# Half products that accumulate in PSUM, weights requested between two spills, copies between token parts: an input projection on one core

## The chip, the cores and the metric

The kernel runs on one core of one Trainium2 chip. The metric is the device time of one execution in microseconds. The program of a core runs on several engines side by side: TensorE (PE, matmuls, with PEld for its weight loads), VectorE (DVE), ScalarE (ACT), GpSimd (POOL), and SyncE (SP), which here only requests DMA transfers. They wait for one another through semaphores.

## What is computed

One inference step of a decoder trunk of two layers, for 1040 prompt rows (16 meta tokens and 1024) and 8 samples of 4 rows, 1072 tokens in all. The layer's input projection is the part that matters here:

```python
hn = _rmsnorm(x, pre_g)
proj = jnp.einsum('bld,de->ble', hn, w_in)      # D_MODEL = 1024 -> EVEN_IN or ODD_IN features
# even layer (A): q, k, v, og, ig, fg, z, xr, gr = split(proj)
#   mLSTM heads on q, k, v, gated by sigmoid(og) and silu(z); RG-LRU on xr, gr
# odd layer (C):  q, k, v, r, alow = split(proj)
#   gated linear attention on q, k, v, gated by silu(r)
mix = ...                                       # the recurrences
y = x + _rmsnorm(jnp.einsum('ble,ed->bld', mix, w_out), post_g)
```

## The kernel before

Each layer has a projection stage and a mixing stage. Every fp32 matrix product is made of three passes over a high and a low part of each operand: high with high, high with low, low with high. The low part is made on DVE by subtracting the high part, which ACT makes by a copy with rounding; this is called a split.

The first tiles of a projection (gates, LRU inputs, q, k) are computed directly (`Projection`, line 471): the features of a tile are 128, the contraction goes over 8 blocks of 128, and the tokens are cut in three. The remaining 32 tiles of 128 features, in each layer, are computed in 16 pairs by `HalfProducts`. A pair is an upper and a lower tile of features. The contraction is cut in two halves, the tokens are cut in two halves, and so a pair is a 2 x 2 block product, which is made from seven half products instead of eight. They are numbered 1 to 7. Products 1 and 2 need the upper weights, products 5, 6 and 3 need the sums of weights, products 7 and 4 need the lower weights and a sum. Each needs a token part: parts 1, 2 and 4 are sums made ahead, part 3 is made last and is stored over a part of the normed tokens (`t3_sum`, `t3_his`, `t3_lows`). One half product is 24 matmuls of 268 columns on line 624: 2 column halves, 4 blocks, 3 passes.

PE takes the products of a pair in the order that `order` gives, and puts them in turn in four places of PSUM of two banks each (`out`). It waits before a product until the one that lay in its place four products ago has been read (`wait_read`). ACT copies product 1 from PSUM (line 650; in pair 0 products 5, 4 and 1), and DVE adds all others (line 657) into the stage tiles `upper` and `lower`. The upper tile is finished by the add of product 3 (or 2), the lower one by that of product 4 (or 7).

For each pair the weights are loaded from HBM (`load`, line 542, two transfers of 512 KB, one for each of the two raw buffers `pa_w_raw` or `pc_w_raw`). `sum_weights` makes three sums on DVE (lines 552 to 557), `split_upper_hi` (ACT, line 565), `split_upper_lo` (DVE, line 569), `split_sums_hi` (ACT, line 575), `split_sums_lo` (DVE, line 579), `split_lower_hi` (ACT, line 587) and `split_lower_lo` (DVE, line 591) split them. A raw buffer may be loaded again when its split and the sums are done.

A finished tile is gated or scaled in place or with a helper tile and then spilled to HBM by two transfers (lines 989 and 990, 2511 and 2512). In layer A the pairs are 4 of kind k (scaled on ACT, line 1131), 4 of og (sigmoid on ACT), 4 of z (sigmoid on ACT, line 1136, then multiplied on DVE, line 1254) and 4 of v (plain). In layer C the first 8 pairs are gated (sigmoid on ACT, line 2601, multiplied on DVE, line 2696), and the last 8 are plain. A stage tile is written again only when its spill has landed.

The order of the work on each engine is written out by hand: `copies` and `finish` for ACT, `sums_of` for DVE, `products` for PE, and the loop over pairs on SP, where the weights of pair p + 1 are requested at the top of pair p, ahead of both of its spills. Ahead of the first of them, in layer A, SP requests three small transfers (lines 1008 to 1010).

Of the kernel before, what the change touches and what calls it, by code (L numbers as in the profile page):

```python
# [35 lines left out]
H = 4  # L36
# [455 lines left out]
class HalfProducts:  # L492
# [100 lines left out]
    def order(self, p):  # L593

        return "1265374" if p else "5412637"
# [114 lines left out]
    def t3_his(self, act):  # L710
        for k in range(KH):
            act.wait_ge(self.t_sum, 3 * KH + k + 1)
            act.activation(self.S.XT_hi[:, k, HC:T], self.temps[2 * (k % 2)], ACT.Copy).then_inc(self.t_hi_ready, 1)
# [11 lines left out]
    def copies(self, act, p, upper, lower):  # L725

        if p == 0:
            act.wait_ge(self.spilled[1], 32 * self.before)
            self.copy(act, p, 5, lower[1])
            self.copy(act, p, 4, lower[0])  # L730
        act.wait_ge(self.spilled[0], 32 * (self.before + p))
        self.copy(act, p, 1, upper[0])

    def sums_of(self, dve, p, upper, lower, more, between):

        def into(x, y, after):

            dve.wait_ge(self.added, after)
            dve.tensor_tensor(x, x, y, ALU.add).then_inc(self.added, 1)
        if p:  # L740
            self.split_lower_lo(dve, p)
            dve.wait_ge(self.copied, 3 + p)
            dve.wait_ge(self.spilled[1], 32 * (self.before + p))
            self.add(dve, p, 6, lower[0], upper[0], 0)
            self.add(dve, p, 2, upper[0], upper[0], 1)
            if more:
                self.split_upper_lo(dve, p + 1)
            self.add(dve, p, 5, lower[1], lower[0], 1)
# [2803 lines left out]
```

## Time and profile before

| | us |
|---|---|
| median of 3 runs | 2098.87 (2097.29 to 2101.58) |
| the profiled execution, its own time | 2098.2 |
| its span, first to last instruction | 2096.4 |
| PE busy with matmuls | 2027.8 (97%) |
| DVE busy | 1239.6 (59%) |
| ACT busy | 798.4 (38%) |
| mean granted clock of TensorE | 0.984 of full |

The profile is of one execution. Its times are counted from the span's start. A row of the timeline gives start, duration, engine, line, operation, output and inputs, and in brackets how long the engine stood idle before it and who ended that. Matmuls overlap in PE, so their durations (0.29 us) are longer than the distance of their starts.

### The profile page before, as it was taken

To read this page: it belongs to the slowest core of one execution; us is meant where nothing else is said; L and a number is where in the kernel's file an instruction comes from. 1 tells how busy PE (TensorE), PEld (TensorE's weight loads), DVE (VectorE), ACT (ScalarE), POOL (GpSimd) and SP (SyncE) were. 2 spreads that over 40 slices of the span, in tenths; PEclk is the share of its full clock that TensorE was granted. 3 is DMA by queue.
4 is the path that set the end of the run, shared out by engine and by line. 5 is a ranking of instruction groups with operands and counts; after the bars stand their busy time and mean duration, and the time that the engine had idled before them with its cause. 6 is when DMAs were issued, how large, how long until landed. Compare 5 with 4: busy or idle time off the path is not lost. (4 is left out here: it accounts for less than half of the span.)

```text
span 2096.4 us, 33284 instructions
## 1 busy us (share of the span) xinstructions
PE 2027.8 (97%) x12862; PEld 1803.7 (86%) x12862; DVE 1239.6 (59%) x2206; ACT 798.4 (38%) x1501; POOL 320.3 (15%) x442
## 2 busy tenths in 40 slices
PE   7999999999999799999979999999999799999998
PEld 7999999999999677787659999999999677777774
DVE  5466676645564666666646557676655465455544
ACT  5555543323231544444345344332212343333323
POOL 0000000000000532242210000000000452323222
PEclk9999999999999999999979999999999899999999
DMA  3121232443333754555332332444433544545442
GB/s 141 56 63 51 65 103 76 149 155 93 114 102 102 244 175 161 173 166 190 102 133 76 98 88 84 139 137 134 117 95 112 181 173 165 183 164 182 161 155 73
DMA packets 211496, 268.92 MB, mean 128 GB/s; under 512 B 49396, under 2 KB 157172, under 8 KB 209304
## 3 DMA queue, kind: packets, MB, share of 16 engines
q1 hardware_dynamic: 211352, 266.95, 39.9%
q8 instruction: 97, 1.59, 0.3%
q14 instruction: 47, 0.39, 0.1%
HBM read 172.72 MB, written 94.18 MB: 127 GB/s over the span
## 5 line engine op out<-in xcount | busy, mean ns | idle before, releaser
L657 DVE TENSOR_TENSOR pa_stage<-pa_ps,pa_stage 128x536 f32<-128x536 f32 x110 | 77.0, 712 | 119.3 <-PE pa_ps L624 111.0
L657 DVE TENSOR_TENSOR pc_stage<-pc_ps,pc_stage 128x536 f32<-128x536 f32 x110 | 77.0, 712 | 100.4 <-PE pc_ps L624 79.3
L471 PE MATMUL pa_ps<-a_XT_hi,pa_w_hi 128*128 128x358 f32 x576 | 133.2, 340 | 0.3 <-PEq L204 0.3
L471 PE MATMUL pa_ps<-a_XT_hi,pa_w_lo 128*128 128x358 f32 x576 | 125.9, 327 | 0.0
L471 PE MATMUL pa_ps<-a_XT_lo,pa_w_hi 128*128 128x358 f32 x576 | 125.8, 326 | 0.0
L624 PE MATMUL pc_ps<-c_XT_hi,pc_w_hi 128*128 128x268 f32 x384 | 110.2, 287 | 0.0
L624 PE MATMUL pa_ps<-a_XT_hi,pa_w_lo 128*128 128x268 f32 x384 | 110.1, 287 | 0.0
L624 PE MATMUL pc_ps<-c_XT_hi,pc_w_lo 128*128 128x268 f32 x384 | 110.1, 287 | 0.0
L624 PE MATMUL pc_ps<-c_XT_lo,pc_w_hi 128*128 128x268 f32 x384 | 110.1, 287 | 0.0
L624 PE MATMUL pa_ps<-a_XT_lo,pa_w_hi 128*128 128x268 f32 x384 | 110.0, 286 | 0.0
L624 PE MATMUL pa_ps<-a_XT_hi,pa_w_hi 128*128 128x268 f32 x384 | 109.8, 286 | 0.0
L1553 PE MATMUL mc_ps<-mc_wout_hi,mc_mix_hi 128*128 128x512 f32 x256 | 105.9, 414 | 4.0 <-POOL mc_mix_lo L3301 4.0
L471 PEld LDWEIGHTS pa_ps<-a_XT_hi,pa_w_hi 128*128 128x128 f32 x576 | 100.2, 189 | 5.9 <-issue 0.6
L1553 PE MATMUL ma_ps<-ma_wout_hi,ma_mix_hi 128*128 128x512 f32 x256 | 104.9, 410 | 0.0
L1553 PE MATMUL mc_ps<-mc_wout_hi,mc_mix_lo 128*128 128x512 f32 x256 | 101.4, 396 | 0.0
L1553 PE MATMUL mc_ps<-mc_wout_lo,mc_mix_hi 128*128 128x512 f32 x256 | 101.0, 394 | 0.0
L1553 PE MATMUL ma_ps<-ma_wout_hi,ma_mix_lo 128*128 128x512 f32 x256 | 100.5, 393 | 0.0
L1553 PE MATMUL ma_ps<-ma_wout_lo,ma_mix_hi 128*128 128x512 f32 x256 | 100.2, 391 | 0.0
L471 PEld LDWEIGHTS pa_ps<-a_XT_hi,pa_w_lo 128*128 128x128 f32 x576 | 99.6, 189 | 0.0
L471 PEld LDWEIGHTS pa_ps<-a_XT_lo,pa_w_hi 128*128 128x128 f32 x576 | 99.4, 189 | 0.0
L3294 POOL TENSOR_TENSOR mc_state<-mc_state,gf 128x512 f32<-128x512 f32 x72 | 74.8, 1060 | 86.8 <-DVE mc_state L3211 86.8
L3211 DVE TENSOR_TENSOR mc_state<-mc_ps,mc_state 128x512 f32<-128x512 f32 x64 | 41.2, 686 | 76.8 <-PE mc_ps L2981 76.1
(581 smaller groups left out, 6000.8 us busy)
## 6 DMA issues: line engine op xcount, KB each, us to landing
pa_w_raw<-in_w_a SPq DMA_DIRECT2D x57, 512.0 KB, 4.6
pc_w_raw<-in_w_c SPq DMA_DIRECT2D x49, 512.0 KB, 4.5
scr_c<-pc_stage SPq DMA_DIRECT2D x48, 512.0 KB, 3.2
scr_a<-pa_stage SPq DMA_DIRECT2D x40, 512.0 KB, 3.2
mc_sample_state<-in_s SPq DMA_DIRECT2D x32, 512.0 KB, 4.6
out_s_s<-mc_sample_state SPq DMA_DIRECT2D x32, 512.0 KB, 2.8
ma_sample_state<-in_c SPq DMA_DIRECT2D x32, 257.0 KB, 4.1
out_c_s<-ma_sample_state SPq DMA_DIRECT2D x32, 257.0 KB, 2.6
```

The costliest lines, as they stand in the source:

```text
L471: ins = pe.matmul(self.ps[:, 3 * s + t, 0:TC], w[:, k, :], x[:, k, t * TC:(t + 1) * TC], start=(k == 0 and j == 0), stop=(k == KT - 1 and ...
L624: ins = pe.matmul(bank[:, half, :], a[:, k, :], b[:, k, cols], start=(k == 0 and j == 0), stop=(k == KH - 1 and j == 2))
L657: dve.tensor_tensor(dst, self.out(p, product), x, ALU.add).then_inc(self.added, 1)
L1553: ins = pe.matmul(ps[:, 6 + half, :], m[:, at, :], w, start=first and j == 0, stop=last and j == 2)
L3211: ins = dve.tensor_tensor(cst[:, n % H, d, :], ps[:, 4 + d, :], cst[:, n % H, d, :], ALU.add)
L3294: ins = pool.tensor_tensor(cst[:, h, d, :], cst[:, h, d, :], factor, ALU.mult)
```

## The change

The half products no longer have four places in turn. In a pair, products 1, 6, 7 and 4 accumulate on top of one another in one place, and products 5 and 3 in another; product 2 has the place that the next pair's product 1 will have. A product that opens a place starts with `start=True`, the others add to what lies there. The order of the products becomes 1 2 6 5 7 3 4, and 5 1 2 6 3 7 4 in pair 0. ACT now copies products 1, 6, 5 and 4, each time the sum so far, and DVE adds products 2, 7 and 3. So a product that adds to a place waits until the sum so far has been read there: 6 for the copy of 1, 7 for the copy of 6, 3 for the copy of 5, 4 for the add of 7.

On ACT a pair is now: the split of its own lower weights, the last step of the pair before, copy 1, the split of the next pair's upper weights, copies 6 and 5, the split of the next sums, the last step of the upper tile, copy 4. In pair 0 it is copy 5, a high part of token part 3, copy 1, another, then the same; two of the four high parts stay ahead of the pairs. On DVE it is the low part of the sums and of the lower weights, the last step of the pair before, add 2, the weight sums of the next pair, add 7, the low part of the next upper weights, add 3 (in pair 0 add 7 comes last).

SP requests the weights of pair 1 where it did before, and those of pair p + 2 between the upper and the lower spill of pair p.

```diff
@@ -592,7 +592,7 @@
 
     def order(self, p):
 
-        return "1265374" if p else "5412637"
+        return "1265734" if p else "5126374"
 
     def at(self, p, product):
 
@@ -600,20 +600,20 @@
 
     def out(self, p, product):
 
-        s = (self.at(p, product) + 1) % 4
+        s = {1: p % 2, 6: p % 2, 7: p % 2, 4: p % 2, 2: 1 - p % 2, 5: 2, 3: 2}[product]
         return self.G.ps[:, 2 * s:2 * s + 2, 0:HC // 2]
 
-    def wait_read(self, eng, p, product):
-
-        copied = {1: 3 + p} if p else {5: 1, 4: 2, 1: 3}
-        added = {6: 1, 2: 2, 5: 3, 3: 4, 7: 6, 4: 7} if p else {6: 1, 2: 4, 3: 5, 7: 7}
-        if product in copied:
-            eng.wait_ge(self.copied, copied[product])
-        else:
-            eng.wait_ge(self.added, 7 * p + added[product])
+    def wait_copied(self, eng, p, what):
+
+        eng.wait_ge(self.copied, 4 * p + ("1654" if p else "5164").index(str(what)) + 1)
+
+    def wait_added(self, eng, p, product):
+
+        eng.wait_ge(self.added, 3 * p + ("273" if p else "237").index(str(product)) + 1)
 
     def product(self, pe, p, product):
 
+        opens = product in (1, 2, 5)
         w, t = {1: ("A11", "B11"), 2: ("A12", "B21"), 3: (2, "B22"), 4: ("A22", 4), 5: (0, 1), 6: (1, 2), 7: ("S3", 3)}[product]
         bank = self.out(p, product)
         passes = [(self.weights(w, lo_w), self.tokens(t, lo_t)) for lo_w, lo_t in ((0, 0), (0, 1), (1, 0))]
@@ -621,17 +621,33 @@
             cols = slice(half * HC // 2, (half + 1) * HC // 2)
             for k in range(KH):
                 for j, (a, b) in enumerate(passes):
-                    ins = pe.matmul(bank[:, half, :], a[:, k, :], b[:, k, cols], start=(k == 0 and j == 0),
-                                    stop=(k == KH - 1 and j == 2))
+                    ins = pe.matmul(bank[:, half, :], a[:, k, :], b[:, k, cols], start=(opens and k == 0 and j == 0),
+                                    stop=(k == KH - 1 and j == 2), skip_group_check=True)
         ins.then_inc(self.done, 1)
 
-    def products(self, pe, p):
+    def products(self, pe, p, hook=None):
         for i, name in enumerate(self.order(p)):
-            q = 7 * p + i
-            if q == 2:
-                pe.wait_ge(self.G.psum_free[0], (self.first + 1) // 2)
-            if q >= 4:
-                self.wait_read(pe, (q - 4) // 7, int(self.order((q - 4) // 7)[(q - 4) % 7]))
+            if i == 4 and hook:
+                hook()
+            if name == "1":
+                if p:
+                    self.wait_added(pe, p - 1, 2)
+                else:
+                    pe.wait_ge(self.G.psum_free[0], (self.first + 1) // 2)
+            elif name == "2":
+                if p:
+                    self.wait_copied(pe, p - 1, 4)
+            elif name == "6":
+                self.wait_copied(pe, p, 1)
+            elif name == "5":
+                if p:
+                    self.wait_added(pe, p - 1, 3)
+            elif name == "7":
+                self.wait_copied(pe, p, 6)
+            elif name == "3":
+                self.wait_copied(pe, p, 5)
+            else:
+                self.wait_added(pe, p, 7)
             if name in "12":
                 pe.wait_ge(self.upper_ready, p + 1)
             elif name in "563":
@@ -644,17 +660,28 @@
                     pe.wait_ge(self.t_ready, 1)
             self.product(pe, p, int(name))
 
-    def copy(self, act, p, product, dst):
-
+    def copy(self, act, p, product, tiles):
+
+        upper, lower = tiles
+        dst, s = {1: (upper[0], 0), 6: (upper[1], 0), 5: (lower[1], 1), 4: (lower[0], 1)}[product]
+        act.wait_ge(self.spilled[s], 32 * (self.before + p))
         act.wait_ge(self.done, self.at(p, product))
         act.activation(dst, self.out(p, product), ACT.Copy).then_inc(self.copied, 1)
 
-    def add(self, dve, p, product, dst, x, after):
-
+    def add(self, dve, p, product, tiles):
+
+        upper, lower = tiles
+        dst, copied = {2: (upper[0], 1), 7: (lower[1], 5), 3: (upper[1], 6)}[product]
+        self.wait_copied(dve, p, copied)
         dve.wait_ge(self.done, self.at(p, product))
-        if after:
-            dve.wait_ge(self.added, 7 * p + after)
-        dve.tensor_tensor(dst, self.out(p, product), x, ALU.add).then_inc(self.added, 1)
+        dve.tensor_tensor(dst, self.out(p, product), dst, ALU.add).then_inc(self.added, 1)
+
+    def wait_tile(self, eng, p, m):
+
+        self.wait_added(eng, p, (3, 7)[m])
+        self.wait_copied(eng, p, (6, 4)[m])
+        if m == 0:
+            self.wait_added(eng, p, 2)
 
     def t_sums(self, dve, i):
 
@@ -722,55 +748,51 @@
         dve.wait_ge(self.t3_used, KH)
         dve.sem_inc(self.t_ready, 1)
 
-    def copies(self, act, p, upper, lower):
-
...
+    def act_pair(self, act, p, tiles, more, finish, after_first=lambda: None, late=lambda: None):
+
         if p:
+            self.split_lower_hi(act, p)
+            finish(p - 1, 1)
+            self.copy(act, p, 1, tiles)
+            after_first()
+        else:
+            self.copy(act, p, 5, tiles)
+            self.t3_his(act, 2)
+            self.copy(act, p, 1, tiles)
+            self.t3_his(act, 3)
+        if more:
+            self.split_upper_hi(act, p + 1)
+        self.copy(act, p, 6, tiles)
+        if p:
+            self.copy(act, p, 5, tiles)
+        late()
+        if more:
+            self.split_sums_hi(act, p + 1)
+        finish(p, 0)
+        self.copy(act, p, 4, tiles)
+        if not more:
+            finish(p, 1)
+
+    def dve_pair(self, dve, p, tiles, more, finish, middle=lambda: None):
+
+        if p:
+            self.split_sums_lo(dve, p)
             self.split_lower_lo(dve, p)
-            dve.wait_ge(self.copied, 3 + p)
-            dve.wait_ge(self.spilled[1], 32 * (self.before + p))
...
+            finish(p - 1, 1)
+        self.add(dve, p, 2, tiles)
+        middle()
+        if more:
+            self.sum_weights(dve, p + 1)
+        if p:
+            self.add(dve, p, 7, tiles)
+        if more:
             self.split_upper_lo(dve, p + 1)
-            self.add(dve, p, 3, upper[1], lower[1], 3)
-            self.sum_weights(dve, p + 1)
...
+        self.add(dve, p, 3, tiles)
+        if not p:
+            self.add(dve, p, 7, tiles)
+        finish(p, 0)
+        if not more:
+            finish(p, 1)
 
 
 A_KINDS = ("k", "og", "z", "v")
@@ -1009,11 +1031,10 @@
                 sp.dma_start(row_d, S.rrow).then_inc(finished, 16)
                 sp.dma_start(gain_d.rearrange("o (k p) -> p (o k)", p=P), S.vecs[:, V_PRE_C:V_PRE_C + KT],
                              allow_slow_non_contiguous=True).then_inc(finished, 16)
+                for s in range(2):
+                    HP.load(sp, 1, s)
                 for p in range(NPAIR):
                     kind, h = kind_of(p)
-                    if p + 1 < NPAIR:
-                        for s in range(2):
-                            HP.load(sp, p + 1, s)
                     if 1 <= p <= w_out.tiles // 2:
                         sp.wait_ge(rows_turned, 1)
                         sp.wait_ge(HP.t_ready, 1)
@@ -1024,8 +1045,12 @@
                             sp.wait_ge(spilled[s], A_SPILLED[0])
                         load_first_head(sp)
                     for m in range(2):
+                        if m and p + 2 < NPAIR:
+                            for s in range(2):
+                                HP.load(sp, p + 2, s)
                         if kind == "v":
-                            spill(HP.added, HP.ready(p)[m], m, h, A_SLOT[kind] + m)
+                            HP.wait_tile(sp, p, m)
+                            spill(HP.done, 7 * p + 6 + m, m, h, A_SLOT[kind] + m)
                         else:
                             spill(final[m], p + 1, m, h, A_SLOT[kind] + m)
                 sp.wait_ge(lru_spilled, 16 * 2 * 8)
@@ -1118,7 +1143,8 @@
                         gate_rows_act_out(act)
                     if k == 6:
                         HP.split_sums_hi(act, 0)
-                HP.t3_his(act)
+                HP.t3_his(act, 0)
+                HP.t3_his(act, 1)
                 act.preload_act_table_set('sigmoid_and_others')
 
                 def finish(p, m):
@@ -1126,7 +1152,7 @@
                     kind, h = kind_of(p)
                     if kind == "v":
                         return
-                    act.wait_ge(HP.added, HP.ready(p)[m])
+                    HP.wait_tile(act, p, m)
                     if kind == "k":
                         act.activation(flat[m][:, 0:T], flat[m][:, 0:T], ACT.Copy, scale=0.0625).then_inc(final[m], 1)
                     elif kind == "og":
@@ -1136,16 +1162,9 @@
                         act.activation(z_sig, flat[m][:, 0:T], ACT.Sigmoid).then_inc(sigmoid_ready, 1)
                 for p in range(NPAIR):
                     more = p + 1 < NPAIR
-                    if p == 3 * H:
+                    if p == 3 * H + 1:
                         act.preload_act_table_set('natural_log_exp_and_others')
-                    HP.copies(act, p, upper, lower)
-                    if more:
-                        HP.split_upper_hi(act, p + 1)
-                        HP.split_sums_hi(act, p + 1)
-                    finish(p, 0)
-                    if more:
-                        HP.split_lower_hi(act, p + 1)
-                    finish(p, 1)
+                    HP.act_pair(act, p, (upper, lower), more, finish)
 
             @block.vector
             def _(dve):
...
@@ -2530,11 +2548,13 @@
                 for i in range(8):
                     pair(i)
                 spill(qk_ready, 16, 0, 3, 3)
+                def next_weights(p):
+                    if p + 2 < NPAIR:
+                        for s in range(2):
+                            HP.load(sp, p + 2, s)
+                next_weights(-1)
                 for p in range(NPAIR):
                     gated, h, d = head_of(p)
-                    if p + 1 < NPAIR:
-                        for s in range(2):
-                            HP.load(sp, p + 1, s)
                     if 1 <= p <= w_out.tiles // 2:
                         sp.wait_ge(HP.t_ready, 1)
                         w_out.load(sp, p - 1)
@@ -2545,10 +2565,14 @@
                         load_first_head(sp)
                     if gated:
                         spill(u_ready, p + 1, 0, h, 8 + d)
+                        next_weights(p)
                         spill(l_ready, p + 1, 1, h, 9 + d)
                     else:
-                        spill(HP.added, HP.ready(p)[0], 0, h, 4 + d)
-                        spill(HP.added, HP.ready(p)[1], 1, h, 5 + d)
+                        for m in range(2):
+                            HP.wait_tile(sp, p, m)
+                            spill(HP.done, 7 * p + 6 + m, m, h, 4 + d + m)
+                            if m == 0:
+                                next_weights(p)
 
             @block.scalar
             def _(act):
...
```

## Rows read from the trace of the kernel before

**Rows 1.** The page, part 1: busy us, share of the span, count.

```profile
PE 2027.8 (97%) x12862; PEld 1803.7 (86%) x12862; DVE 1239.6 (59%) x2206; ACT 798.4 (38%) x1501; POOL 320.3 (15%) x442
```

**Rows 2.** Windows of both layers' half products, line 624 alone.

```profile
core 0: us, PE busy (x) PEld busy (x), PEclk, DMA share, GB/s
354.00:687.40 333.40, 333.33 (x2687) 333.14 (x2688) 1.00 0.38 116
1304.60:1637.80 333.20, 332.92 (x2688) 332.74 (x2688) 1.00 0.39 119
```

**Rows 3.** Windows of two pairs of layer A; after PEld come DVE, ACT, POOL.

```profile
541.70:562.60 20.90, 20.90 (x171) 20.90 (x170) 14.10 (x17) 6.36 (x7) 0.00 (x0) 1.00 0.35 103
...
666.70:687.40 20.70, 20.70 (x169) 20.70 (x168) 6.78 (x9) 1.68 (x2) 0.00 (x0) 1.00 0.19 54
```

**Rows 4.** Timeline of PE in layer C's pair 0.

```profile
1316.92 0.39 PE L624 MATMUL pc_ps<-pc_t_hi,pc_w_sums_hi 128*128 128x268 f32 x1 [0.24 <-ACT pc_stage L650]
```

**Rows 5.** Timeline of PE, first matmul of the half products in A and C.

```profile
353.99 0.29 PE L624 MATMUL pa_ps<-pa_t_hi,pa_w_sums_hi 128*128 128x268 f32 x1
...
1304.63 0.29 PE L624 MATMUL pc_ps<-pc_t_hi,pc_w_sums_hi 128*128 128x268 f32 x1
```

**Rows 6.** Timeline of ACT in layer A's pair 0: the next pair's upper split.

```profile
372.07 1.06 ACT L565 ACTIVATE pa_w_hi<-pa_w_raw 128x1024 fp32r<-128x1024 f32 x1 [5.51 <-DMA pa_w_raw<-in_w_a]
```

**Rows 7.** Timeline of SP ahead of layer A's pair 1.

```profile
358.78 0.39 SPq L1010 DMA_DIRECT2D scr_g<-vecs  x1
```

**Rows 8.** The tile view of pa_w_raw, window 359 to 365: requests and landings.

```profile
L542 SPq DMA_DIRECT2D pa_w_raw<-in_w_a x2: 363/440/517, 359.3 to 359.9; - x2
...
DMA to landing us min/median/max: 12.8/13.1/13.5
```

**Rows 9.** Timeline of DVE in pair 0 of A (three) and C (one).

```profile
355.34 1.22 DVE L569 TENSOR_TENSOR pa_w_lo<-pa_w_raw,pa_w_hi 128x1024 fp32r<-128x1024 f32 x1 [3.65 <-ACT pa_w_hi L565]
...
374.93 0.68 DVE L552 TENSOR_TENSOR pa_w_sums<-pa_w_raw 128x512 f32<-128x512 f32 x1
...
377.46 1.33 DVE L657 TENSOR_TENSOR pa_stage<-pa_ps,pa_stage 128x536 f32<-128x536 f32 x2
...
1307.25 1.22 DVE L569 TENSOR_TENSOR pc_w_lo<-pc_w_raw,pc_w_hi 128x1024 fp32r<-128x1024 f32 x1
```

**Rows 10.** Timeline of ACT at the end of one pair of layer A.

```profile
414.30 1.49 ACT L575 ACTIVATE pa_w_sums_hi<-pa_w_sums 128x1536 fp32r<-128x1536 f32 x1 [7.93 <-DVE pa_w_sums L557]
415.69 1.08 ACT L1131 ACTIVATE pa_stage<-pa_stage 128x1072 f32<-128x1072 f32 x1
417.04 1.06 ACT L587 ACTIVATE pa_w_hi<-pa_w_raw 128x1024 fp32r<-128x1024 f32 x1 [0.26 <-PE pa_ps L624]
```

**Rows 11.** Timeline of DVE and SP in layer C: a gate, its spill, the spill's landing.

```profile
1353.14 1.33 DVE L2696 SCALAR_TENSOR_TENSOR pc_stage<-pc_stage,vecs,first_head_c 128x1072 f32<-128x1072 f32 x1 [1.17 <-ACT first_head_c L2601]
...
1358.06 1.53 DVE L657 TENSOR_TENSOR pc_stage<-pc_ps,pc_stage 128x536 f32<-128x536 f32 x2 [2.21 <-DMA scr_c<-pc_stage]
...
1354.50 0.37 SPq L2511 DMA_DIRECT2D scr_c<-pc_stage  x1
```

**Rows 12.** Timeline of SP and ACT in layer A: the slowest upper spill.

```profile
585.47 0.38 SPq L989 DMA_DIRECT2D scr_a<-pa_stage  x1
...
590.61 0.62 ACT L650 ACTIVATE pa_stage<-pa_ps 128x536 f32<-128x536 f32 x1 [3.09 <-DMA scr_a<-pa_stage]
```

**Rows 13.** PE's timeline after a long gap, and windows with the granted clock.

```profile
1663.62 0.80 PE L1553 MATMUL mc_ps<-mc_wout_hi,mc_mix_hi 128*128 128x512 f32 x1 [4.03 <-POOL mc_mix_lo L3301]
...
1665.50:1668.90 3.40, 3.40 (x9) 2.31 (x7) 0.00 (x0) 0.00 (x0) 3.40 (x6) 0.50 0.00 0
1669.00:1672.40 3.40, 3.40 (x21) 2.49 (x21) 1.67 (x3) 0.26 (x1) 2.86 (x6) 1.00 0.00 0
...
1316.00:1320.00 4.00, 3.76 (x31) 3.54 (x30) 0.00 (x0) 2.82 (x5) 0.00 (x0) 1.00 0.00 0
```

**Rows 14.** The page, part 6: requests, count, KB each, median us to landing.

```profile
pa_w_raw<-in_w_a SPq DMA_DIRECT2D x57, 512.0 KB, 4.6
```

More of the change, by code:

```diff
@@ L708, in t3_sum, with t3_his @@
         dve.tensor_tensor(x, x, y, ALU.add).then_inc(self.t_sum, 1)
[L710 to L713, printed above, removed]
+    def t3_his(self, act, k):
+        act.wait_ge(self.t_sum, 3 * KH + k + 1)
+        act.activation(self.S.XT_hi[:, k, HC:T], self.temps[2 * (k % 2)], ACT.Copy).then_inc(self.t_hi_ready, 1)
     def t3_lows(self, dve):
@@ L723, in t3_lows @@
         dve.sem_inc(self.t_ready, 1)
-    def copies(self, act, p, upper, lower):
[L727 to L739, printed above, removed]
-        if p:
-            self.split_lower_lo(dve, p)
-            dve.wait_ge(self.copied, 3 + p)
-            dve.wait_ge(self.spilled[1], 32 * (self.before + p))
-            self.add(dve, p, 6, lower[0], upper[0], 0)
-            self.add(dve, p, 2, upper[0], upper[0], 1)
-            if more:
-                self.split_upper_lo(dve, p + 1)
-            self.add(dve, p, 5, lower[1], lower[0], 1)
-            self.add(dve, p, 3, upper[1], lower[1], 3)
-            if more:
-                self.sum_weights(dve, p + 1)
-            self.add(dve, p, 7, lower[1], lower[1], 4)
-            self.add(dve, p, 7, lower[0], lower[0], 3)
-        else:
-            dve.wait_ge(self.copied, 3)
-            self.add(dve, p, 6, upper[1], upper[0], 0)
-            into(lower[1], upper[1], 1)
-            into(lower[0], upper[1], 1)
-            self.add(dve, p, 2, upper[0], upper[0], 1)
-            self.split_upper_lo(dve, p + 1)
-            self.add(dve, p, 3, upper[1], lower[1], 3)
-            self.sum_weights(dve, p + 1)
-            self.add(dve, p, 7, lower[1], lower[1], 5)
-            self.add(dve, p, 7, lower[0], lower[0], 3)
-        if more:
-            self.split_sums_lo(dve, p + 1)
-        between()
-        if p:
-            self.add(dve, p, 4, lower[0], lower[0], 6)
@@ L771, in ready @@
-    def ready(self, p):
-        return 7 * p + 4 if p else 5, 7 * p + 7
+    def act_pair(self, act, p, tiles, more, finish, after_first=lambda: None, late=lambda: None):
+        if p:
+            self.split_lower_hi(act, p)
[19 more added lines that the diff above has]
+            finish(p, 1)
@@ L1258, in _ @@
                 for p in range(NPAIR):
-                    if p and kind_of(p - 1)[0] == "z":
-                        z_gate(p - 1, 1)
-                    HP.sums_of(dve, p, upper, lower, p + 1 < NPAIR,
-                               (lambda: z_gate(p, 0)) if kind_of(p)[0] == "z" else (lambda: None))
+                    HP.dve_pair(dve, p, (upper, lower), p + 1 < NPAIR, z_gate)
             @block.gpsimd
@@ L2594, in _, with sigmoid @@
                 HP.split_upper_hi(act, 0)
[L2595 removed]
+                HP.t3_his(act, 0)
+                HP.t3_his(act, 1)
                 act.preload_act_table_set('sigmoid_and_others')
[L2598 to L2601 removed]
+                def sigmoid(p, m):
+                    if head_of(p)[0]:
+                        HP.wait_tile(act, p, m)
+                        act.wait_ge(sig_read, 2 * p + m)
+                        act.activation(sig, flat[m][:, 0:T], ACT.Sigmoid).then_inc(sig_ready, 1)
                 for p in range(NPAIR):
                     gated, h, d = head_of(p)
[L2604 removed]
+                    if p == 9:
                         act.preload_act_table_set('natural_log_exp_and_others')
[L2606 to L2616 removed]
+                    HP.act_pair(act, p, (upper, lower), p + 1 < NPAIR, sigmoid)
             @block.vector
@@ L2689, in _, with gate @@
                 HP.t3_lows(dve)
-                def gate(p, m, x):
+                def gate(p, m):
                     gated, h, d = head_of(p)
+                    if not gated:
+                        return
+                    x = flat[m]
                     dve.wait_ge(sig_ready, 2 * p + m + 1)
@@ L2701, in _ @@
                 for p in range(NPAIR):
-                    if p and head_of(p - 1)[0]:
-                        gate(p - 1, 1, flat[1])
-                    HP.sums_of(dve, p, upper, lower, p + 1 < NPAIR, (lambda: gate(p, 0, flat[0])) if head_of(p)[0] else (lambda: None))
+                    HP.dve_pair(dve, p, (upper, lower), p + 1 < NPAIR, gate)
             @block.tensor
```

21 lines of the change are left out of this document (2 added, 19 removed).

## The prediction

> **What bounds the kernel now.** I read the page's busy line first: the TensorE (PE) has work for 97% of the span [rows 1]. The reader is to see that a change can gain only where PE stands still, and can lose wherever it makes PE stand still. Then I cut out the two stretches that the change touches, the half products of both layers (line 624), with the windows view: 333.40 us and 333.20 us with 333.33 and 332.92 us of matmul in them [rows 2]. So at most 0.07 + 0.28 = 0.35 us of idle can be removed there. In layer C's pair 0 PE's timeline names one wait, 0.24 us, for an ACT copy [rows 4]. A third look is at single pairs: VectorE (DVE) is busy 14.10 of 20.90 us in one and 6.78 of 20.70 us in another, and PE starts its matmuls at the same pace in both (171 in 20.90 us, 169 in 20.70 us) [rows 3]. Taking adds off DVE gives PE nothing. Hence the working is about one question: which waits does the new order put in front of PE?
>
> One unit is needed throughout: 333.4 us / 2688 matmuls = 0.124 us, so a product (24 matmuls) takes 2.98 us and a pair (7 products) 20.83 us.
>
> **Removed work.** A pair loses four DVE adds and gets three ScalarE (ACT) copies more. An add takes 0.72 us, of two in a row the second starts about 0.62 us after the first (line 657, 1.33 us for two) [rows 9]; a copy takes 0.62 us [rows 12]. Both lie under 20.83 us of matmul, with DVE and ACT idle for a third of it or more [rows 3]: worth nothing. If the cover were gone, three copies would cost 1.9 us a pair.
>
> **Pair 0 of layer A, product 7.** PE starts at 353.99 [rows 5]; the new order is 5 1 2 6 3 7 4, so product 7 is due at 353.99 + 5 x 2.98 = 368.87. It now accumulates where product 6 lies, so it waits for ACT's copy of 6. In ACT's queue that copy stands behind the split of the next pair's upper weights (line 565), and ACT's rows stand in the order of its program. In the trace that split starts at 372.07, after 5.51 us of waiting for the weights' transfer [rows 6]. The transfer isn't moved: it is requested at 359.3 and 359.9, behind the small transfers that end with the one of line 1010 [rows 7], and lands 12.8 and 13.5 us later [rows 8], so at 372.1 and 373.4. Before, nothing that PE needed soon stood behind it. Now: split 372.07 to 373.13, its successor starting about 0.1 us before its end as in [rows 10] (414.30 + 1.49 against 415.69), copy 373.03 to 373.65, PE about 0.05 us later, at 373.7. Stall: 373.7 - 368.87 = 4.8 us.
>
> **The same pair, product 4.** It accumulates where product 7 has just been written, so it waits for DVE's add of 7, the last product before it. That add has 2.98 us of cover in later pairs, where product 3 stands between, and none in pair 0. Product 7 ends at 373.7 + 2.98 = 376.7. DVE has to do the next pair's weight sums first, which need both transfers: from 373.4, 2.53 us as in the trace (374.93 to 377.46), then the upper weights' low part (about 1.15 us), add 3 (0.62 us until the next starts), add 7 (0.72 us) [rows 9]: 373.4 + 2.53 + 1.15 + 0.62 + 0.72 = 378.4. PE goes on at 378.5 instead of 376.7: 1.8 us more. Together 4.8 + 1.8 = 6.6 us.
>
> **Pair 0 of layer C.** Here the weights are requested without small transfers ahead, and nothing waits for them. Product 1 moves from third place to second and needs the upper weights' low part, which DVE starts at 1307.25 and ends 1.22 us later [rows 9]: 1308.5 against 1304.63 + 2.98 = 1307.6 [rows 5]; 0.9 us. Layer A has the same step, but there the part is ready at 355.34 + 1.22 = 356.56 [rows 9], before product 1 is due at 356.97. Product 4 again waits for add 7, with nothing in between: an engine hears of PE's end 0.26 us after it [rows 10], the add takes 0.72 us, the way back some 0.05 us: 1.0 us. Sum for C: 1.9 us.
>
> **The clock.** An idle PE of 4.8 us has no like in these stages, but has one later: PE waits 4.03 us and goes on at 1663.62, and in 1665.50 to 1668.90 the granted clock is 0.50 (1.2 of 2.4 GHz); at 1669.00 it is 1.00 again [rows 13]. The short gap in layer C (0.24 us idle [rows 4]) left 1.00 around it [rows 13]. So I take half clock for the same 1669.0 - 1663.6 = 5.4 us after product 7 starts: 21.8 of its 24 matmuls at twice 0.124 us, 2.2 at 0.124, end 379.4 instead of 376.7. The add of 7 is free by then, and product 4 starts at 379.4 + 0.26 + 0.72 + 0.05 = 380.4, 1.9 us later than without. Bounds: 0 (clock kept) and 1.9 us; I take 1.9, since the gap of 4.03 us is the nearest row. The gaps of 0.9 and 1.0 us in C I put at no loss of clock, by the row around C's gap.
>
> **Every later pair.** With start T, product 6 is third, due at T + 5.95, and waits for the copy of product 1, which waits until the pair before has spilled its upper tile. In the gated pairs (8 in C, 4 of z in A) that chain starts at product 3's end, now the sixth, at T - 2.98: +0.26 to ACT, the sums' split (1.39 us until the next start), sigmoid 1.08 [rows 10], the gate on DVE 1.33, then the spill's request (1354.50 for a gate that began at 1353.14, so 1.36) [rows 11]. Request: T - 2.98 + 0.26 + 1.39 + 1.08 + 1.36 = T + 1.1. From the request to the wait's end it is 3.56 us where two weight transfers follow at once, as they will now [rows 11]: T + 4.7, copy 0.62, T + 5.35. Cover left: 0.6 us, so no stall. One landing in the trace took 5.14 us (585.47 to 590.61) [rows 12]; such a one would cost 5.14 - 3.56 - 0.6 = 1.0 us. I put this at 0, with 12 x 0.4 = 5 us as its upper bound for transfers that slow each other by 1 us.
>
> The request of weights between the two spills stands on the sync queue (SP) ahead of the lower spill. It waits for the lower weights' split, which DVE ends at about T + 4.1 (after the gate's end at T + 1.1, the low part of the sums, an estimated 1.8 us from 1.22 us for two thirds of the elements, then 1.22 us [rows 9]); the lower tile's gate follows and ends at T + 5.4, so nothing is held there. An ungated tile is held some 3 us, but its buffer is needed only by the copy of product 5 at T + 11.9 + 0.26, and the spill lands by T + 9. The weights land about T + 9, and their sums (2.53 us) end before DVE's add of 7 is due at T + 15.1. Nothing queued there is late.
>
> **The stages' ends.** The last step is a copy of 0.62 us in place of an add of 0.72 us: -0.1 us at each, left out.
>
> **Sum.** 6.6 + 1.9 (A) + 1.9 (C) - 0.35 (idle of before removed) = 10.05 us. The profiled execution took 2098.2 us (span 2096.4 and 1.8 around it), 0.67 us under the median of the runs shown and inside their spread. 2098.2 + 10.05 = 2108.
>
> **Rivals.**
>
> *The weights come in time (no change).* If both landed before 368.87 - 0.67 - 0.96 = 367.2 (the copy with its way to PE, and the split), product 7 would start on time. Left are add 7 in both layers (1.0 each) and product 1 in C (0.9), minus 0.35: +2.6 us, 2101. For it: such a transfer's median landing is 4.6 us [rows 14]. Against: what stands ahead of this one is not touched. Landings up to about 1.5 us later still stay below the 0.2% (4.2 us) that a measurement of this kernel can tell from no change.
>
> *A quicker PE (faster).* Place: line 624, 5376 matmuls at 0.124 us each, if DVE's reads of PSUM slowed PE. Its price: each nanosecond per matmul is 5.4 us; it decides from (10.05 + 4.2) / 5376 = 2.7 ns on, and at 4 ns it gives 2098.2 + 10 - 21.5 = 2087 us. Against: the same pace with DVE 14.10 and 6.78 us busy [rows 3].
>
> *PE stops in every gated pair (much slower).* If the spill's landing grows by 1 us beside the weights, 12 pairs lose 0.4 us each: 2113. If such small stops also took the clock down, each would cost up to 5.4 / 2 = 2.7 us more, 12 x 2.7 = 32 us: 2145. Against: the short gap in C left the clock at 1.00 [rows 4, 13]. The Trainium skill ("TensorE: Matmul & The Clock Gate", section "A second HAM failure mode: psum-queue depth-cycling") tells of a kernel whose PSUM places were cycled so that short PE pauses between groups made the clock swing between half and full; that would be this second case. The trace's short gap doesn't bear it out, its long one does.
>
> **Chances and range.** Forecast (some 5 to 14 us slower): 0.68. Every gated pair stops: 0.09, of which the clock's case 0.03. Weights in time or nearly: 0.16. Quicker PE: 0.07. The likeliest is 2108; without the clock 2106.2; with landings 1 us earlier or later 2105 to 2109; with the gated pairs' bound 2113. The range is 2102 to 2113: it takes in part of the second case, and leaves out the quicker PE and the clock's 32 us. Slower by over 0.2%: 0.68 + 0.09 = 0.77; within: 0.16; faster: 0.07.
>
> **What the changed profile would show.** Right: in layer A's pair 0 one PE gap of about 5 us that ends with ACT's copy, ACT idle before line 565 until about 372 for the weights; a second gap of 1 to 2 us that ends with DVE's add; two gaps of 0.9 and 1.0 us in C's pair 0; a granted clock of 0.50 for some microseconds after the first gap; pairs 1 to 15 of 20.83 us. Wrong: weights of pair 1 that land before 367, another pace of line 624, or PE gaps before product 6 in gated pairs.

## The result, and the profile after

The changed kernel takes 2107.42 us (median of 9 runs, 2103.0 to 2110.03) against 2099.18 us of the kernel before on the same chip (9 runs, 2097.29 to 2101.58). The ratio is 1.004 with an interval of 1.003 to 1.005: 8.2 us slower, against a forecast of 10 us. The profiled execution took 2104.3 us with a span of 2102.6.

The page's busy line of the kernel after answers to [rows 1]: DVE has 80 us less work, ACT 53 us more, and PE the same.

```profile
PE 2027.6 (96%) x12862; PEld 1804.6 (86%) x12862; DVE 1159.1 (55%) x2078; ACT 851.7 (41%) x1593; POOL 319.6 (15%) x442
```

The windows view of the half products, line 624 alone, answers to [rows 2]. First layer A, then layer C.

```profile
core 0: us, PE busy (x) PEld busy (x), PEclk, DMA share, GB/s
354.30:696.60 342.30, 336.63 (x2688) 336.10 (x2688) 0.99 0.39 113
1312.10:1647.50 335.40, 333.68 (x2688) 333.21 (x2688) 1.00 0.40 117
```

The reader is to see two things in A's row. The stretch is 8.9 us longer than before, but PE is busy for 3.3 us of that: it stood still for some of the time and went slowly for the rest. In C's row only 2.2 us are added, 1.4 of them idle.

For exact lengths I take the distance from the first to the last start of a matmul of line 624. A goes from 333.41 to 342.02 us, C from 333.12 to 335.18. That is 8.61 + 2.06 = 10.67 us. All later lengths are measured like this.

The waits of PE after, over the whole of A's stretch and then of C's, are four rows. The columns are who waited for whom, us in total, times, and the longest.

```profile
PE pa_ps L624 <- ACT pa_stage L669: 4.7, 1, 4.7
PE pa_ps L624 <- DVE pa_stage L677: 0.9, 1, 0.9
...
PE pc_ps L624 <- DVE pc_stage L677: 0.9, 1, 0.9
PE pc_ps L624 <- issue: 0.8, 1, 0.8
```

Each happens once. So all of the loss by waiting sits in two pairs of 32. PE's timeline after shows them, in pair 0 of A (four rows) and pair 0 of C (two):

```profile
369.13 0.29 PE L624 MATMUL pa_ps<-a_XT_hi,pa_w_sums_lo 128*128 128x268 f32 x1
374.15 0.59 PE L624 MATMUL pa_ps<-a_XT_hi,pa_w_hi 128*128 128x268 f32 x1 [4.73 <-ACT pa_stage L669]
...
379.45 0.31 PE L624 MATMUL pa_ps<-a_XT_hi,pa_w_lo 128*128 128x268 f32 x1
380.64 0.39 PE L624 MATMUL pa_ps<-pa_t_hi,pa_w_hi 128*128 128x268 f32 x1 [0.88 <-DVE pa_stage L677]
...
1316.07 0.36 PE L624 MATMUL pc_ps<-c_XT_hi,pc_w_hi 128*128 128x268 f32 x1 [0.80 <-issue]
...
1332.08 0.39 PE L624 MATMUL pc_ps<-pc_t_hi,pc_w_hi 128*128 128x268 f32 x1 [0.88 <-DVE pc_stage L677]
```

The row at 374.15 is product 7, that at 380.64 product 4, that at 1316.07 product 1, that at 1332.08 product 4 again. A wait put down to "issue" names nobody. That product 1 waits for the low part of the upper weights has to come from DVE's row (1314.74 + 1.23 = 1315.97, 0.1 us before PE goes on).

What product 7 waited for stands in ACT's timeline after, in pair 0 of A.

```profile
372.54 1.06 ACT L565 ACTIVATE pa_w_hi<-pa_w_raw 128x1024 fp32r<-128x1024 f32 x1 [8.56 <-DMA pa_w_raw<-in_w_a]
373.50 0.60 ACT L669 ACTIVATE pa_stage<-pa_ps 128x536 f32<-128x536 f32 x1
```

The copy at 373.50 is that of product 6. It stood behind a split, for which ACT idled 8.56 us until the landing of a transfer that the copy doesn't need. Product 6 had begun its last matmul at 366.13, so the copy stood some 7 us. DVE's timeline for the same time shows the low part of the upper weights (376.36), then the adds of 3 and of 7:

```profile
376.36 1.22 DVE L569 TENSOR_TENSOR pa_w_lo<-pa_w_raw,pa_w_hi 128x1024 fp32r<-128x1024 f32 x1
377.49 0.71 DVE L677 TENSOR_TENSOR pa_stage<-pa_ps,pa_stage 128x536 f32<-128x536 f32 x1
379.87 0.72 DVE L677 TENSOR_TENSOR pa_stage<-pa_ps,pa_stage 128x536 f32<-128x536 f32 x1 [1.66 <-PE pa_ps L624]
...
1314.74 1.23 DVE L569 TENSOR_TENSOR pc_w_lo<-pc_w_raw,pc_w_hi 128x1024 fp32r<-128x1024 f32 x1
```

The clock at the gap is in windows of all engines of the kernel after (PEclk is the third number from the end). It is 1.00 until 372.60 and 0.50 from 372.70 on, while PE still stands. In 374.20 to 379.30 the clock is 0.50 and PE starts 23 matmuls; before, the same window has 44 at 1.00 (last row).

```profile
370.00:372.60 2.60, 0.00 (x0) 0.00 (x0) 0.00 (x0) 0.06 (x1) 0.00 (x0) 1.00 0.89 263
372.70:374.10 1.40, 0.00 (x0) 0.00 (x0) 0.28 (x1) 1.40 (x2) 0.00 (x0) 0.50 0.18 73
374.20:379.30 5.10, 5.10 (x23) 5.10 (x24) 3.97 (x6) 2.55 (x2) 0.00 (x0) 0.50 0.01 3
...
374.20:379.30 5.10, 5.10 (x44) 5.10 (x43) 4.76 (x9) 1.72 (x2) 0.00 (x0) 1.00 0.00 0
```

**The stretches carry the verdict, not the whole.** The span outside the two stretches holds work that the change hardly touches (two high parts of token part 3 move out of it, on ACT). It was 1429.9 us before, 1425.4 after, and 1427.7 to 1433.0 in the eight experiments below (span minus both lengths). It goes with how long the granted clock stands at half in it: the two shortest of the ten profiles (after, and experiment 6) have 57.4 and 54.2 us at half clock there, the one before 65.6, and the longest (experiment 4) 84.0. Two windows of all engines show a part of this, the first 40 us of C's mixing stage. Before:

```profile
1637.80:1677.80 40.00, 29.29 (x127) 22.27 (x127) 20.92 (x37) 19.23 (x40) 25.86 (x47) 0.74 0.66 227
```

After:

```profile
1647.40:1687.40 40.00, 28.63 (x137) 21.84 (x139) 22.03 (x39) 21.56 (x44) 27.52 (x49) 0.83 0.72 254
```

Why the clock differs from execution to execution stays open, and so does whether it accounts for all of the difference. In this pair of profiles it hides 4.5 of the 10.67 us.

### The profile page after: what moved, and what is told of

The parts are those of the page before. It is cut to its first block and busy times, and to the rows that moved or that the text cites. A ratio compares the mean times of both kernels' runs of the same rounds, so it can differ in the third digit from the quotient of the medians.

```text
span 2102.6 us, 33282 instructions
## 1 busy us (share of the span) xinstructions
PE 2027.6 (96%) x12862; PEld 1804.6 (86%) x12862; DVE 1159.1 (55%) x2078; ACT 851.7 (41%) x1593; POOL 319.6 (15%) x442
## 5 line engine op out<-in xcount | busy, mean ns | idle before, releaser
L677 DVE TENSOR_TENSOR pa_stage<-pa_ps,pa_stage 128x536 f32<-128x536 f32 x48 | 34.4, 717 | 114.0 <-PE pa_ps L624 113.8
L677 DVE TENSOR_TENSOR pc_stage<-pc_ps,pc_stage 128x536 f32<-128x536 f32 x48 | 34.4, 717 | 112.0 <-PE pc_ps L624 111.8
L669 ACT ACTIVATE pc_stage<-pc_ps 128x536 f32<-128x536 f32 x64 | 39.7, 620 | 114.6 <-PE pc_ps L624 95.2
```

The source lines that it names most:

```text
L677: dve.tensor_tensor(dst, self.out(p, product), dst, ALU.add).then_inc(self.added, 1)
```

## The experiments

The theory is that of the prediction: queue order in pair 0, weights that land late, and half a clock after the gap. Rivals are that a product on a place just read costs PE something in every pair, and that the weights' earlier request is to blame.

**1. The weights of pair 1 ahead of the small transfers.**

```diff
+                for s in range(2):
+                    HP.load(sp, 1, s)
                 sp.wait_ge(rows_ready, 1)
                 ...
                 sp.dma_start(gain_d.rearrange("o (k p) -> p (o k)", p=P), S.vecs[:, V_PRE_C:V_PRE_C + KT],
                              allow_slow_non_contiguous=True).then_inc(finished, 16)
-                for s in range(2):
-                    HP.load(sp, 1, s)
```

> The changed kernel, but in layer A the weights of pair 1 are requested ahead of the three small transfers (row and gain outputs) instead of behind them. Stretch of the half products in A (first to last matmul): 333.4 us before, 342.0 us in the changed kernel. Theory (pair 1's late landing holds ACT's copy of 6, and then DVE's sums hold the add of 7): the weights land about 363, both long waits go, only the add of 7 (1.0 us) is left; A takes 334.8 us, the whole 2100 to 2103 us. Rival (accumulating in PSUM costs a little in every pair, the late weights are a coincidence): A stays at 340 us or more, the whole at 2105 or more.

Measured: 2099.86 us, ratio to before 1.0006 (0.9998 to 1.0015). A is 334.67, C 335.40. The tile view of `pa_w_raw`, the loads ahead of pair 1, says after:

```profile
DMA to landing us min/median/max: 12.9/13.1/13.3
```

and in this experiment:

```profile
DMA to landing us min/median/max: 4.3/4.5/4.8
```

So the order of requests on one queue is worth 8.6 us of landing and 342.02 - 334.67 = 7.35 us of PE. Left in A is one gap of 1.17 us for the add of 7. The rival by which each pair costs something falls, but for some 0.02 us a pair: the other 15 pairs of A follow the same new order here.

**2. The copy of 6 ahead of the split, in pair 0.**

```diff
+        if not p:
+            self.copy(act, p, 6, tiles)
         if more:
             self.split_upper_hi(act, p + 1)
-        self.copy(act, p, 6, tiles)
+        if p:
+            self.copy(act, p, 6, tiles)
```

> The changed kernel, but in pair 0 ACT copies product 6 ahead of the split of pair 1's upper weights. Theory (two queues are held by the same landing): product 7 starts on time, but product 4 then waits for DVE's add of 7, which stands behind the weight sums until about 378.8, 6.6 us after it is due, and the clock falls there instead; A stays at 341.5 to 342.5 us, no gain. Rival (ACT's queue alone is at fault): the gap of 5.0 us goes, with the half clock after it; A takes 335 to 337 us, the whole 2101 or so.

Measured: 2106.49 us, ratio 1.0042 (1.0028 to 1.0056). A is 343.15, 0.65 us over the upper end expected. Mending ACT's queue alone gains nothing: product 7 is on time, and the wait goes one product further, from ACT to DVE. PE's timeline of this experiment:

```profile
379.16 0.59 PE L624 MATMUL pa_ps<-pa_t_hi,pa_w_hi 128*128 128x268 f32 x1 [6.87 <-DVE pa_stage L677]
```

The same late transfer now holds the add of 7, behind the weight sums in DVE's queue. The clock falls as well, later (window of all engines):

```profile
374.40:384.60 10.20, 5.44 (x24) 5.44 (x25) 6.34 (x8) 2.58 (x2) 0.00 (x0) 0.50 0.37 105
```

**3. Both queues mended.** DVE as well does what waits for no weights first. The part of `dve_pair` that changes:

```diff
+        if not p:
+            self.add(dve, p, 3, tiles)
+            self.add(dve, p, 7, tiles)
+            self.split_upper_lo(dve, p + 1)
         if more:
             self.sum_weights(dve, p + 1)
         if p:
             self.add(dve, p, 7, tiles)
-        if more:
-            self.split_upper_lo(dve, p + 1)
-        self.add(dve, p, 3, tiles)
-        if not p:
-            self.add(dve, p, 7, tiles)
+            if more:
+                self.split_upper_lo(dve, p + 1)
+            self.add(dve, p, 3, tiles)
```

> As the kernel with copy 6 first, and in pair 0 DVE adds products 3 and 7 and makes the upper weights' low part ahead of the next pair's weight sums. Theory: product 7 is on time, product 4 waits 1.0 us for its add, product 2 of pair 1 some 1.1 us for the copy of 4, which stands behind the late sums' split on ACT; A takes about 335.6 us, the whole 2101 to 2104. Rival (a cost in every pair): A at 340 or more.

Measured: 2109.47 us, ratio 1.0051 (1.0036 to 1.0065). A is 336.70, C 339.70. In A the theory held: 5.3 us came back with the transfer as late as ever (13.0 to 13.5 us). The rest are a gap of 1.17 us between starts in pair 0 (add 7) and gaps of 1.39 and 0.67 us in pair 1, 1.1 us more in all than expected. In C, and so in the whole, the expectation failed. There the weights had not been late, and the sums, now made after the adds, were. ACT's row for their split in pair 0 of C, and PE's waits for ACT in C:

```profile
1331.83 1.49 ACT L575 ACTIVATE pc_w_sums_hi<-pc_w_sums 128x1536 fp32r<-128x1536 f32 x1 [8.84 <-DVE pc_w_sums L557]
...
PE pc_ps L624 <- ACT pc_stage L669: 2.3, 2, 1.8
```

In the changed kernel the same split starts 7.6 us earlier against the start of the stretch. In pair 1 of C gaps of 0.76 and 2.07 us between starts follow, with some 3.4 us at half clock after the second. So the order of `sum_weights` and the adds matters by which of the two is ready, and one order for both layers doesn't do.

**4. PE kept busy through the gap.** 36 matmuls into a bank that no half product uses stand ahead of product 7 in A's pair 0; their results are read by nothing.

```diff
             elif name == "7":
+                if p == 0 and self.before == 4:
+                    pe.wait_ge(self.lower_ready, 1)
+                    a, b = self.weights("A22", 0), self.tokens("B22", 0)
+                    for n in range(36):
+                        pe.matmul(self.G.ps[:, 6, 0:HC // 2], a[:, n % KH, :], b[:, n % KH, 0:HC // 2],
+                                  start=True, stop=True, skip_group_check=True)
                 self.wait_copied(pe, p, 6)
```

> The changed kernel with 36 matmuls more (268 columns, into two otherwise unused banks, results not read) ahead of product 7 of A's pair 0, which fill 4.5 of its 5.0 us wait. Theory (the wait takes TensorE's clock down, which costs about 1.8 us on top): product 7's matmuls start 0.124 us apart instead of 0.224, product 4 starts at about 378.9 instead of 380.6, A takes 340.3 us. Rival (the half clock has another cause, or costs nothing beside DVE's late add): A stays at 342.0 us.

Measured: 2109.97 us, ratio 1.0057 (1.0043 to 1.0072). A is 340.73, 1.29 us less than the change alone; C is 336.09, 0.9 us more. PE's timeline of this experiment, products 7 and 4:

```profile
375.30 0.39 PE L624 MATMUL pa_ps<-a_XT_hi,pa_w_hi 128*128 128x268 f32 x1 [0.69 <-ACT pa_stage L675]
...
380.05 0.39 PE L624 MATMUL pa_ps<-pa_t_hi,pa_w_hi 128*128 128x268 f32 x1 [1.49 <-DVE pa_stage L683]
```

Product 7 now takes 2.97 us from its first start to its last (375.30 to 378.27), a full-clock product, and the wait for add 7 is longer in turn. From the start of product 7 to that of product 4 it is 4.75 us here and 6.49 after (374.15 to 380.64). So in the change the clock cost 1.74 us. Of these, 0.45 is lost again, since the weights landed that much later after their request here (ACT's split starts 13.33 us after it, against 12.88). The whole is not lower than with the change: the span outside the stretches is 1433.0 us here, the longest of all, with the most half clock. Why is open; by the whole this experiment says nothing.

**5. The weights requested where they were before**, at the top of the pair ahead.

```diff
                 for p in range(NPAIR):
                     ...
+                    if p + 1 < NPAIR:
+                        for s in range(2):
+                            HP.load(sp, p + 1, s)
```

The loads between the spills are taken out, in both layers.

> The changed kernel, but the weights of pair p + 1 are requested at the top of pair p, after the lower spill of the pair before, as in the kernel before the change. Theory (the new order on ACT needs the early request): in the gated pairs the spill is requested at T + 5.4, the weights at T + 6.5 and 7.0, they land at T + 11.0 and 11.5, the split holds ACT's copy of 6 until T + 12.6, and product 7, due at T + 11.9, waits some 0.7 us in each of 8 pairs in C and 3 or 4 in A; C's stretch grows from 335.2 to about 341 us, A's from 342.0 to about 345, the whole to 2114 us or more. Rival (the early request is not needed, its transfers were hidden before): both stretches stay within 1 us.

Measured: 2120.85 us, ratio 1.0101 (1.0081 to 1.012). A is 346.25, C 343.17. So the earlier request does no harm. It is what the new order needs, and is worth 4.2 us in A and 8.0 us in C. In A 3.4 of these are stops before product 7 in pairs 9 to 12, and 0.5 us is pair 0, where the weights landed some 0.4 us later than in the changed kernel. In C 7.3 are stops before product 7 in pairs 2 to 8, 0.8 to 1.4 us each where 0.7 was expected. One pair of C shows why. SP, ACT and PE of this experiment:

```profile
1366.18 0.37 SPq L2527 DMA_DIRECT2D scr_c<-pc_stage  x1
1366.59 0.58 SPq L2528 DMA_DIRECT2D scr_c<-pc_stage  x1
1367.28 1.56 SPq L542 DMA_DIRECT2D pc_w_raw<-in_w_c  x2
...
1371.90 1.06 ACT L565 ACTIVATE pc_w_hi<-pc_w_raw 128x1024 fp32r<-128x1024 f32 x1 [5.94 <-DMA pc_w_raw<-in_w_c]
1372.86 1.11 ACT L669 ACTIVATE pc_stage<-pc_ps 128x536 f32<-128x536 f32 x2
...
1373.52 0.39 PE L624 MATMUL pc_ps<-c_XT_hi,pc_w_hi 128*128 128x268 f32 x1 [0.78 <-ACT pc_stage L669]
```

The request waits in SP's queue for the lower spill. The split on ACT waits for its landing, the copy of 6 waits behind the split, and product 7 waits for the copy.

**6. Experiment 1, with the two short waits of pair 0 cut in halves.** The add of 7 is made by column halves, so that the first overlaps product 7's second half. The low part of the upper weights is made in two parts, so that product 1 waits for the first alone. The core on PE's side:

```diff
+            if p == 0 and product == 4 and half:
+                self.wait_added(pe, 0, 7)
             for k in range(KH):
                 ...
+            if p == 0 and product == 7 and not half:
+                ins.then_inc(self.t_ready, 1)
```

> The kernel with pair 1's weights ahead of the small transfers, and in pair 0 two waits split by halves: the add of 7 is made for each half of the columns, so that the first half's add runs under the second half of product 7, and the low part of the upper weights is made for product 1's contraction blocks first. Theory (these two waits are all that is left of the loss beside some 0.02 us a pair): A takes 333.6 us (333.4 before), C 333.5 us (333.1 before), the whole is within 0.1% of the kernel before. Rival (a cost is left that the list of waits doesn't name): A or C stays above 334.3 us.

Measured: 2098.61 us, ratio 0.9999 (0.999 to 1.0008). A is 333.53, C 333.63, against 333.41 and 333.12 before. Windows of the half products, which are line 631 here:

```profile
354.00:687.80 333.80, 333.71 (x2688) 333.69 (x2688) 1.00 0.40 115
1304.30:1638.10 333.80, 333.41 (x2688) 333.15 (x2688) 1.00 0.40 118
```

Product 1 of C's pair 0, which waited for nobody by name, now comes 0.66 us after the matmul before it rather than 1.09 (1.31 in experiment 1): so it was the low part that it waited for. With the four waits of pair 0 gone or shortened, the new scheme is as fast as the old one, and no faster. DVE's 80 us less gain nothing.

**7. All four high parts of token part 3 ahead of the copies**, on top of experiment 1, as they stood before.

```diff
-                HP.t3_his(act, 0)
-                HP.t3_his(act, 1)
+                for k in range(KH):
+                    HP.t3_his(act, k)
```

The calls for blocks 2 and 3 between the copies are taken out.

> The kernel with pair 1's weights ahead of the small transfers, with all four high parts of token part 3 made ahead of the pairs' copies on ACT, as before the change. Theory (the copies among the token parts are needed once product 6 waits for the copy of 1): product 6 of pair 0 waits some 3 us in each layer; A takes 337.8 us or more (334.7 without), C 338.2 or more (335.4 without), up to 2 us more each where the clock falls. Rival (the place of these copies doesn't matter, as it didn't before the change): both within 0.5 us.

Measured: 2111.41 us, ratio 1.0054 (1.0038 to 1.0069). A is 339.48 (334.67 in experiment 1), C 339.61 (335.40). PE's timeline, product 6:

```profile
366.22 0.39 PE L624 MATMUL pa_ps<-pa_t_hi,pa_w_sums_hi 128*128 128x268 f32 x1 [3.01 <-ACT pa_stage L669]
```

So moving two of the high parts between the copies saves some 4.5 us a layer in the new order, in which product 6 waits for a copy. A part of that is half clock after the gap.

**8. The small transfer made twice**, ahead of pair 1's weights. The second copy of the gains is read by nothing.

```diff
-                sp.dma_start(gain_d.rearrange("o (k p) -> p (o k)", p=P), S.vecs[:, V_PRE_C:V_PRE_C + KT],
-                             allow_slow_non_contiguous=True).then_inc(finished, 16)
+                for to in (gain_d, nc.dram_tensor("scr_g_again", [1, D], F32, kind="Internal").ap()):
+                    sp.dma_start(to.rearrange("o (k p) -> p (o k)", p=P), S.vecs[:, V_PRE_C:V_PRE_C + KT],
+                                 allow_slow_non_contiguous=True).then_inc(finished, 16)
```

> The changed kernel with the small transfer of the gain row (4 KB in elements of 4 bytes) made a second time, into a scratch row that nothing reads, so that two of them stand ahead of pair 1's weights. Theory: the weights land as much later as that transfer takes, an estimated 6 to 7 us, and PE's gap before product 7 grows from 5.0 to about 11.5 us; A takes about 348.5 us. Rival (the gap has another cause): A stays at 342 us.

Measured: 2118.29 us (one run). A is 350.79. PE's timeline, product 7:

```profile
385.12 0.59 PE L624 MATMUL pa_ps<-a_XT_hi,pa_w_hi 128*128 128x268 f32 x1 [14.51 <-ACT pa_stage L669]
```

The tile view, landings of pair 1's weights:

```profile
DMA to landing us min/median/max: 21.7/22.0/22.3
```

The direction is right, the size was not: the second transfer costs 8.9 us of landing and 9.8 us of PE's gap, where 6 to 7 were expected.

## Why the prediction was right

**The mechanism and its place.** Right. Product 7 was to start at 373.7 and started at 374.15. It was due at 368.87 and, with PE's first matmul 0.37 us later than before (354.36 against 353.99), at 369.2. The stall is 5.02 us between starts, 4.9 more than their usual distance, against 4.8 forecast. Experiments 1 and 8 show the transfer's queue as the cause, experiment 2 that two queues carry it to PE.

**Product 4 and the clock.** Right in sum. The forecast was 1.8 us without the clock's fall or 3.7 with it. Product 4 was due 8.4 us earlier than it came, against 4.8 + 1.8 + 1.9 = 8.5. The granted clock stood at 0.50 from 372.66 to 379.48, so product 7's matmuls came 0.224 us apart rather than 0.124, and product 7 ended near 379.5, as forecast (379.4). Experiment 4 takes the clock's part away and shows its price, 1.74 us against 1.9 forecast. Without it product 4 comes 4.75 us after product 7, against 378.5 - 373.7 = 4.8. That the length fits so well is partly luck. From PE's first matmul to the full clock it took 5.3 us here, against 5.4 taken from one row; after the other gaps that took the clock down it was 3.0 us (experiment 8) to 5.5 us (experiments 2 and 5).

**Pair 0 of C.** 0.97 and 1.04 us more than the usual distance of starts (gaps of 1.09 and 1.16), against 0.9 and 1.0. The clock stays at 1.00 through both, as taken.

**Later pairs.** Taken as 0, bound 5 us. They stand at 20.85 us in A (20.83 before) and 20.82 in C (20.79 before): 0.02 to 0.03 us a pair, 0.7 us in all, which the forecast didn't have; where they come from no run here shows. Against them stands that more was removed than the 0.35 us of idle. Between starts, the old order lost 0.32 us in A's pair 1 (21.15 us against 20.83) and 0.41 us at the matmul of [rows 4], and the new one loses neither. The two misses nearly cancel, and that is luck too. No gap stands before product 6: the time from the spill's request to the copy was 3.84 and 3.74 us in the two pairs that ACT's and SP's timelines of C show, against 3.56 taken. The margin was thin. In experiment 4 one slower landing made a gap of 0.69 us before product 6.

**The order of requests on SP.** "Nothing queued there is late" was right: in pair 2 of C the two spills are requested at T + 1.17 and T + 5.46, against T + 1.1 and T + 5.4. And experiment 5 shows what the words left out: the request had to move. The forecast took the change as a whole and gave its parts no price. To the old order an earlier request and copies between the token parts can have been worth less than 1 us, since all its stops together took no more. To the new order they are worth 12.2 and some 9 us.

**The rivals.** Weights in time: experiment 1 makes that world, and gives 334.67 + 335.40 - 666.53 = 3.5 us in the stretches, against 2.6. A quicker PE: no; the matmuls of gapless pairs keep their pace with 80 us less on DVE. PE stopping in every gated pair: not in the change. Experiment 5 has short stops, with 1.0 to 1.6 us between starts, before product 7 in seven pairs of C in a row. The windows view of its half products says of C:

```profile
1316.70:1660.10 343.40, 335.37 (x2688) 333.39 (x2688) 1.00 0.37 115
```

The clock stays at 1.00. The case that the prediction took from the Trainium skill ("TensorE: Matmul & The Clock Gate", section "A second HAM failure mode: psum-queue depth-cycling"), with a clock that swings when PE pauses between groups, doesn't show at these pauses.

**The whole.** 8.2 us against 10.05. The forecast lies inside the measured interval (6.3 to 10.5 us). The stretches gave 10.67 in one pair of profiles, so no step of the sum was far off. Where the 2.4 us between these and the medians went isn't shown; the rest of the program varies by 7.6 us over the ten profiles.

## What to carry to other kernels

When a result accumulates on a place that must be read first, the reader's whole queue becomes part of PE's path: look for what stands ahead of that read in the queue, and for what that in turn waits for. A product between the one that is read and the one that accumulates on it hides the read; where there is none, the read by halves hides most of it. Parts of such a change are not priced alone: here two parts that could gain the old order next to nothing saved 12 and 9 us in the new one.

## What was not expected of the hardware

Three small transfers ahead of two weight loads of 512 KB on the same queue made these land 12.9 to 13.3 us after their request rather than 4.3 to 4.8. The last of the three is that of the gains (4 KB, written element by element). A second one of that kind made it 21.7 to 22.3 us, so nearly all of the delay can be put down to it; no run moves the other two alone.

The half clock came before the gap was over: the granted clock was 0.50 from 372.66 on, while PE started again at 374.15 after 5.02 us between starts. After a gap of 2.07 us between starts (experiment 3, layer C) and after gaps of 3.30 and 2.93 us (experiment 7, layers A and C) it stood at half for some 3.4 us; after those of 1.0 to 1.6 us (experiment 5, layer C) not at all. Windows of all engines, one of experiment 3 and two of experiment 7:

```profile
1341.40:1344.70 3.30, 3.30 (x17) 3.30 (x16) 0.74 (x2) 1.20 (x2) 0.00 (x0) 0.50 1.03 335
...
367.60:370.90 3.30, 3.30 (x17) 3.30 (x16) 2.98 (x4) 0.00 (x0) 0.00 (x0) 0.50 0.00 0
1323.40:1326.70 3.30, 3.30 (x16) 3.30 (x17) 3.27 (x6) 0.71 (x1) 0.00 (x0) 0.50 0.00 0
```
